# First expert pairs: order of the weight pieces on VectorE, and the tables of further visits on GpSimd

## The reference, cut to what matters

```python
def moe_swiglu(xn, router, wg, wu, wd):
    xt = xn.reshape(B * T, D)
    logits = (xt @ router).astype(F32)
    topv, topi = lax.top_k(logits, TOP_K)
    gates = jax.nn.softmax(topv, axis=-1)
    combine = jnp.sum(jax.nn.one_hot(topi, N_EXPERTS, dtype=F32) * gates[..., None], axis=1)
    y = jnp.zeros((B * T, D), F32)
    for e in range(N_EXPERTS):
        y = y + combine[:, e:e + 1] * swiglu(xt, wg[e], wu[e], wd[e]).astype(F32)
    return y.reshape(B, T, D).astype(xn.dtype)
```

## Time and profile before

| | |
|---|---|
| median of 3 runs | 2581.31 us |
| the profiled execution | 2579.01 us, its span 2577.2 us |
| TensorE matmul busy | 2502.2 us, 97% of the span |
| VectorE busy | 1932.0 us, 75% |
| ScalarE busy | 1492.6 us, 58% |
| GpSimd busy | 58.4 us, 2% |
| chain that ended last | PE 86%, DVE 8%, ACT 3%, DMA 2% |
| the 672 lo parts of L2306 | 798.3 us, 1226 ns each |
| the 672 hi parts of L2196 | 702.8 us, 1062 ns each |

### The profile page before, as it was taken

One profiled execution on the slowest core, in us unless ns is written; L12 is line 12 of the kernel. 1 busy time (PEld: TensorE's weight loads), 2 busy tenths in 40 slices (PEclk: granted clock), 3 DMA queues, 4 the chain that ended last, 5 costly groups with the idle time before them and its releaser, 6 DMA issues.

```text
span 2577.2 us, 41939 instructions
## 1 busy us (share of the span) xinstructions
PE 2502.2 (97%) x15981; PEld 2118.4 (82%) x15981; DVE 1932.0 (75%) x2704; ACT 1492.6 (58%) x2152; POOL 58.4 (2%) x32
## 2 busy tenths in 40 slices
PE   8899999989999999999999999999999999999998
PEld 7676998857888888888888888857999999866998
DVE  7855556758999999999999987877656655677555
ACT  5513434456888888888788885392443433356432
POOL 0100000000001010100001000000000000000000
PEclk9999999999999999999999999999999999999999
DMA  6655542587999999999999994203544552321551
GB/s 262 244 210 230 191 185 109 222 340 283 373 357 378 357 376 361 364 369 366 370 365 368 366 353 191 115 1 141 197 177 177 192 181 90 112 117 76 219 184 52
DMA packets 90971, 619.82 MB, mean 241 GB/s; under 512 B 10208, under 2 KB 10464, under 8 KB 40800
## 3 DMA queue, kind: packets, MB, share of 16 engines
q1 hardware_dynamic: 88992, 609.17, 61.5%
q0 software_dynamic: 1280, 4.72, 0.5%
q10 hardware_dynamic: 576, 4.19, 0.5%
HBM read 615.95 MB, written 2.10 MB: 240 GB/s over the span
## 4 chain that ended last, share of the span: by engine, by line
PE 86%; DVE 8%; ACT 3%; DMA 2%; issue 1%; DVEq 0%; SPq 0%; ACTq 0%
PE psum L1952 8%; PE psum L1954 8%; PE psum L1953 8%; PE psum L387 6%; PE psum L389 6%; PE psum L388 6%; PE psum L1989 4%; PE psum L1987 4%; PE psum L1988 4%; PE psum L402 3%; PE psum L403 3%; PE psum L404 3%; DMA ring<-stream_dram 2%; PE psum L1442 1%; PE psum L1961 1%; PE psum L2494 1%
## 5 line engine op out<-in xcount | busy, mean ns | idle before, releaser
L2306 DVE TENSOR_TENSOR r_high<-ring,r_high 128x1024 fp32r<-128x1024 f32 x672 | 798.3, 1226 | 56.6 <-ACT r_high L2196 43.6
L2196 ACT ACTIVATE r_high<-ring 128x1024 fp32r<-128x1024 f32 x672 | 702.8, 1062 | 75.9 <-PE psum L1954 49.7
L387 PE MATMUL psum<-r_low,r_high 128*128 128x256 f32 x1408 | 399.8, 284 | 1.5 <-DVE r_high L473 1.1
L389 PE MATMUL psum<-r_low,r_high 128*128 128x256 f32 x1408 | 398.4, 283 | 0.0
L1952 PE MATMUL psum<-r_high 128*128 128x512 f32 x896 | 359.1, 401 | 0.9 <-DVE r_high L2297 0.9
L1954 PE MATMUL psum<-r_high 128*128 128x512 f32 x896 | 349.8, 390 | 0.0
L1953 PE MATMUL psum<-r_high 128*128 128x512 f32 x896 | 349.4, 390 | 0.0
L473 DVE TENSOR_TENSOR r_high<-ring,r_high 128x1024 fp32r<-128x1024 f32 x264 | 307.1, 1218 | 9.5 <-ACT r_high L435 9.3
L388 PE MATMUL psum<-r_high 128*128 128x256 f32 x1056 | 298.8, 283 | 0.0
L447 ACT ACTIVATE arena<-psum 128x256 f32<-128x256 f32 x88 | 33.8, 384 | 441.0 <-PE psum L389 438.2
L387 PEld LDWEIGHTS psum<-r_low,r_high 128*128 128x128 f32 x1408 | 269.9, 192 | 6.6 <-DVE r_high L473 1.3
(11 more groups left out here) (603 smaller groups left out, 4468.5 us busy)
## 6 DMA issues: line engine op xcount, KB each, us to landing
ring<-stream_dram SPq DMA_DIRECT2D x160, 1536.0 KB, 6.5
ring<-stream_dram SPq DMA_DIRECT2D x224, 1024.0 KB, 6.8
ring<-stream_dram SPq DMA_DIRECT2D x224, 512.0 KB, 6.3
arena<-bias_dram ACTq DMA_DIRECT2D x2, 1024.0 KB, 7.7
pack<-pack_dram SPq DMA_DIRECT2D x1, 1664.0 KB, 16.9
const<-const_dram SPq DMA_DIRECT2D x1, 1060.0 KB, 13.4
x<-x_dram SPq DMA_DIRECT2D x1, 1024.0 KB, 4.9
xc<-ctx_dram ACTq DMA_DIRECT2D x1, 1024.0 KB, 6.2
```

Of the source, the lines that this page charges most:

```text
L387: pe.matmul(dst, hi, f["x_hi"][:, k, :], start=(k == 0), stop=False)
L389: ins = pe.matmul(dst, lo, f["x_hi"][:, k, :], start=False, stop=(k == KD - 1))
L2196: act.activation(dst, src, ACT.Copy).then_inc(sem("moe_w_hi"), 1)
L2306: ins = dve.tensor_tensor(lo, src, hi.bitcast(f32), SUB)
```

## The change

The function that makes lo parts is renamed to moe_split_lo, and takes any engine; it is still called for VectorE only. In moe_first_dve the order is new: own pieces 1 and 2, then both row operations, then xe_lo of half 0; and the product (moe_hidden_dve) stands behind pieces 0 and 1 of the next pair, with the next pair's pieces 2 and 3 and own pieces 4 and 5 behind it. The tables of further visits leave VectorE and are made by GpSimd ahead of its loop, with other operations: the sum over 8 experts as three additions in place of a reduction, one further visit at a time. VectorE waits for them once (pool_out) behind stage 13 of visit 0, and TensorE's wait for gathered rows counts one more (POOL_LRU).

```diff
@@ -1862,7 +1862,7 @@
         gates, chosen = tables[:, 272:280], tables[:, 280:296]
         ss_rest, root_bias = sm("ss_rest", 1), sm("root_bias", 1)
         xe_hi, xe_lo = [parts(27648 + D * i, D, "p (k s) -> p k s", k=KD) for i in range(2)]
-        AHEAD, POOL_LRU = 4, 2
+        AHEAD, POOL_LRU = 4, 3
         INDEX_AT, GATHER_AT = 6, 8
         x_rows = nc.dram_tensor("x_rows", (NT * P, D), f32).ap()
         slot_x = ar(0, D)
...
@@ -2095,7 +2095,7 @@
             add(1, 1)
             route_turned_dve(dve, 1)
             route_rows_dve(dve, 1, "norm_xn")
-            moe_split_dve(dve, moe_at(0, 0), 0, 0, 1)
+            moe_split_lo(dve, moe_at(0, 0), 0, 0, 1)
             route_choice_dve(dve, 1)
             best = top.rearrange("p (j e) -> p e j", j=NT)
             S(dve.tensor_tensor(gts[:, 2:4], best[:, 1, :], best[:, 0, :], SUB))
...
@@ -2258,6 +2258,8 @@
             pool.wait_ge(sem("norm_xn"), 4)
             pool.dma_start(x_rows.rearrange("(j p) d -> p j d", p=P), x_tm).then_inc(sem("moe_rows_in"), 16)
             moe_weights_pool(pool)
+            moe_more_visits_pool(pool)
+            moe_more_values_pool(pool)
             n_more = moe_more(pool)
             pool.wait_ge(sem("moe_rows_in"), 16)
             with pool.Fori(0, n_more) as v:
...
@@ -2296,14 +2298,14 @@
             dve.wait_ge(sem("moe_xe_hi"), half + 1)
             dve.tensor_tensor(xe_lo[:, ks, :], xe[:, ks, :], xe_hi[:, ks, :].bitcast(f32), SUB).then_inc(sem("moe_xe"), 1)
 
-        def moe_split_dve(dve, at, p, first=0, end=6):
+        def moe_split_lo(eng, at, p, first=0, end=6):
             r, turn, pair = at
             for q in range(first, end):
                 src = piece_of(r, q)
                 hi, lo = [steps_of(w[:, 0, :], 2 * q, 2) if q < 4 else d[:, 2 * (p % 2) + q - 4, :]
                           for w, d in ((wp_hi, d_hi), (wp_lo, d_lo))]
-                dve.wait_ge(sem("moe_w_hi"), 6 * pair + (q + 1))
-                ins = dve.tensor_tensor(lo, src, hi.bitcast(f32), SUB)
+                eng.wait_ge(sem("moe_w_hi"), 6 * pair + (q + 1))
+                ins = eng.tensor_tensor(lo, src, hi.bitcast(f32), SUB)
                 if q < 2:
                     ins.then_inc(sem("moe_w_lo"), 1)
                 elif q in (3, 5):
...
@@ -2353,54 +2355,56 @@
             S(pool.tensor_copy(token_of[:, :, 1], inv_rms[:, 0:2]))
             step(pool, pool.tensor_copy(gate_t[:, 0:2], vwgt[:, 0:2]), "moe_tables")
 
-        def moe_more_visits_dve(dve):
-
-            def S(ins, name="dve_step"):
-                step(dve, ins, name)
+        def moe_more_visits_pool(pool):
+
+            def S(ins, name="pool_step"):
+                step(pool, ins, name)
             iota8 = cst("iota")[:, 0:N_EXP]
             extra = MAX_VISITS - N_EXP
-            S(dve.tensor_tensor(rank, rank, over, SUB))
+            pool.wait_ge(sem("moe_plan"), 1)
+            S(pool.tensor_tensor(rank, rank, over, SUB))
             for n in range(extra):
-                S(dve.scalar_tensor_tensor(which[:, n, :], rank, float(n), over, ALU.is_equal, MUL))
-            S(dve.tensor_tensor(which_tmp[:, 0:extra, :], which, iota8.unsqueeze(1).to_broadcast([P, extra, N_EXP]), MUL))
-            S(dve.tensor_reduce(plan_f[:, 9:9 + extra], which_tmp[:, 0:extra, :], AX.X, ADD))
-            S(dve.tensor_copy(plan_f[:, 1:9], iota8))
-            S(dve.tensor_copy(plan_i[:, 1:12], plan_f[:, 1:12]), "moe_plan")
-
-        def moe_more_values_dve(dve, pairs):
-
-            def S(ins, name="dve_step"):
-                step(dve, ins, name)
+                S(pool.tensor_scalar(which[:, n, :], rank, float(n), None, ALU.is_equal))
+                S(pool.tensor_tensor(which[:, n, :], which[:, n, :], over, MUL))
+                S(pool.tensor_tensor(which_tmp[:, 0, :], which[:, n, :], iota8, MUL))
+                for e in (4, 2, 1):
+                    S(pool.tensor_tensor(which_tmp[:, 0, 0:e], which_tmp[:, 0, 0:e], which_tmp[:, 0, e:2 * e], ADD))
+                S(pool.tensor_copy(plan_f[:, 9 + n:10 + n], which_tmp[:, 0, 0:1]))
+            S(pool.tensor_copy(plan_f[:, 1:9], iota8))
+            S(pool.tensor_copy(plan_i[:, 1:12], plan_f[:, 1:12]), "moe_plan")
+
+        def moe_more_values_pool(pool):
+
+            def S(ins, name="pool_step"):
+                step(pool, ins, name)
             extra = MAX_VISITS - N_EXP
-            for dst, src in pairs:
-                for j in range(NT):
-                    S(dve.tensor_tensor(which_tmp[:, extra * j:extra * (j + 1), :], which,
-                                        src[:, :, j].unsqueeze(1).to_broadcast([P, extra, N_EXP]), MUL))
-                S(dve.tensor_reduce(dst[:, 2 * N_EXP:2 * MAX_VISITS].rearrange("p (n j) -> p j n", j=NT),
-                                    which_tmp.rearrange("p (j n) e -> p j n e", j=NT), AX.X, ADD))
-            if dst is vwgt:
-                S(dve.tensor_scalar(vpos[:, 2 * N_EXP:2 * MAX_VISITS], vpos[:, 2 * N_EXP:2 * MAX_VISITS], -float(CAP),
-                                    None, ADD))
+            for dst, src in ((vsel, sel), (vpos, pos), (vwgt, wgt)):
+                for n in range(extra):
+                    own = which_tmp[:, 0:NT, :]
+                    S(pool.tensor_tensor(own, which[:, n, :].unsqueeze(1).to_broadcast([P, NT, N_EXP]),
+                                         src.rearrange("p e j -> p j e"), MUL))
+                    for e in (4, 2):
+                        S(pool.tensor_tensor(own[:, :, 0:e], own[:, :, 0:e], own[:, :, e:2 * e], ADD))
+                    S(pool.tensor_tensor(dst[:, 2 * (N_EXP + n):2 * (N_EXP + n) + NT], own[:, :, 0], own[:, :, 1], ADD))
+            step(pool, pool.tensor_scalar(vpos[:, 2 * N_EXP:2 * MAX_VISITS], vpos[:, 2 * N_EXP:2 * MAX_VISITS], -float(CAP),
+                                          None, ADD), "pool_out")
 
         def moe_first_dve(dve):
 
             own, nxt = moe_at(0, 0), moe_at(0, 1)
-            moe_split_dve(dve, own, 0, 1, 2)
+            moe_split_lo(dve, own, 0, 1, 3)
             moe_xe_rows_dve(dve, 0)
-            moe_split_dve(dve, own, 0, 2, 3)
+            moe_xe_rows_dve(dve, 1)
             moe_xe_lo_dve(dve, 0)
-            moe_xe_rows_dve(dve, 1)
-            moe_split_dve(dve, own, 0, 3, 4)
+            moe_split_lo(dve, own, 0, 3, 4)
             moe_xe_lo_dve(dve, 1)
-            moe_split_dve(dve, nxt, 1, 0, 1)
-            moe_split_dve(dve, own, 0, 4, 5)
-            moe_split_dve(dve, nxt, 1, 1, 3)
+            moe_split_lo(dve, nxt, 1, 0, 2)
             moe_hidden_dve(dve, own)
-            moe_split_dve(dve, nxt, 1, 3, 4)
-            moe_split_dve(dve, own, 0, 5, 6)
+            moe_split_lo(dve, nxt, 1, 2, 4)
+            moe_split_lo(dve, own, 0, 4, 6)
             dve.wait_ge(sem("moe_h_hi"), 1)
             moe_hidden_lo_dve(dve)
-            moe_split_dve(dve, nxt, 1, 4, 6)
+            moe_split_lo(dve, nxt, 1, 4, 6)
 
         def moe_hidden_dve(dve, at):
             dve.wait_ge(sem("moe_silu"), at[2] + 1)
...
@@ -2427,10 +2431,8 @@
                         moe_pick_dve(dve, v + 1, p - 3)
                     if more and p in (5, 6):
                         moe_gate_dve(dve, v + 1, p - 5)
-                    if first and p == 7:
-                        moe_more_visits_dve(dve)
-                    if first and p in (8, 9, 10):
-                        moe_more_values_dve(dve, (((vsel, sel), (vpos, pos), (vwgt, wgt))[p - 8],))
+                    if first and p == PAIRS - 1:
+                        dve.wait_ge(sem("pool_out"), POOL_LRU)
                 if more:
                     moe_stage_dve(dve, moe_at(v, PAIRS), moe_at(v, PAIRS + 1), 0, out=v)
                 else:
```

More of the change, by code:

```diff
@@ L2313, in moe_stage_dve @@
             if nxt is not None:
-                moe_split_dve(dve, nxt, p + 1, 0, 3)
+                moe_split_lo(dve, nxt, p + 1, 0, 3)
             moe_hidden_dve(dve, at)
@@ L2319, in moe_stage_dve @@
             if nxt is not None:
-                moe_split_dve(dve, nxt, p + 1, 3, 5)
+                moe_split_lo(dve, nxt, p + 1, 3, 5)
             if out is not None:
@@ L2332, in moe_stage_dve @@
             if nxt is not None:
-                moe_split_dve(dve, nxt, p + 1, 5, 6)
+                moe_split_lo(dve, nxt, p + 1, 5, 6)
         def moe_out_dve(dve, v):
```

## The result

The changed kernel takes 2592.37 us, the median of 6 runs (2587.35 to 2595.13); the kernel before, measured beside it, 2581.30. The ratio is 1.0037, with a 95% interval from 1.0026 to 1.0047: by that ratio 9.6 us slower, by the medians 11.1. The forecast was 2581.4. The profiled execution took 2588.59 us with a span of 2586.8, against 2579.01 and 2577.2 before.

A forecast was written before the change was run, and what follows sets the result against it. VectorE was taken to pace the experts' first visit, with TensorE full almost everywhere after 612 us. Order +1.4, tables off VectorE -1.5 and GpSimd holding VectorE +0.2 summed to +0.1: 2581.4 us, range 2578.6 to 2592.0.

The forecast's parts named there:

- Part 3: Tables on GpSimd: 61 small operations done near 655, needed by 669.8, so cover 15 us and cost 0.
- the clock falls: Rival: the new 2.3 us TensorE hole could bring half clock for 3 us, costing 1.5: 2582.9; chance 0.05.
- Nine pieces between the products: VectorE, first to second pair's product: two pieces added make 9, 10.9 us instead of 8.6.
- Shift by the order 1.4: Part of the new moe_first_dve order: second pair's transposes 1.4 us later, and the shift stays 1.4.
- No further stall: Third pair: gate-up and TensorE both come 1.4 us later, so the shift does not grow.
- Tables off VectorE -1.5: Stage 7: without 3.08 us of tables the product precedes TensorE, closing the hole at 682.25; gain 1.5 us.
- GpSimd holding VectorE 0.2: Small GpSimd operations delay VectorE in the bound stretch 611 to 622: between 0 and 1.9 us, taken as 0.2.
- GpSimd done near 655: GpSimd's 61 table operations get in at ends of VectorE pieces, some 9 in 8.6 us, from 602.
- The sum of +0.1: Whole kernel: +1.4 for the order, -1.5 for the tables, +0.2 for GpSimd holding VectorE; 2581.4 us.
- The gather comes late: Rival: GpSimd tables finish near 680, delaying visit 1's gathered rows and TensorE's transposes by 10 us: 2591.5; chance 0.24.
- the forecast's own line of 5.2 us: A measurement tells 0.2% (5.2 us) from no change; chances faster 0.03, same 0.73, slower 0.24.
- three marks of being wrong: Second pair's transposes at 620 or before, a table operation beyond 670, or TensorE waiting for GpSimd at p = 8.

The follow-up runs named there:

- e1: The changed kernel with GpSimd's last visit-table operation raising moe_plan by itself, so each engine has its own count; ratio to the kernel before 1.0005.
- e5: The changed kernel with GpSimd's cast of the visit indices moved behind all but the last of the 37 value operations; ratio to the kernel before 1.0078.
- e9b: The changed kernel with 8 idle TensorE matmuls before the first gate-up and one before the first transposes; ratio to the kernel before 1.0032.
- e3: The kernel before with only the new order of moe_first_dve, tables still on VectorE; ratio to the kernel before 1.0011.
- e7: The kernel before with only the new order's second half, the first pair's product two pieces earlier; ratio to the kernel before 1.0011.
- e2: e1 with moe_first_dve in the old order, so only the tables move to GpSimd; ratio to the kernel before 0.9994.
- e4: e1 with another VectorE order: own pieces fill its waits, 7 pieces between the products; 2580.80 us, ratio to the kernel before 0.9996.
- e10: The kernel before with only idle TensorE matmuls around the gather and in the first pair's waits; ratio to the kernel before 0.9995.
- e4b: The same program as e4, measured again; ratio to the kernel before 0.9993.

## Why the prediction was wrong in its time and right in its parts

**The step that failed** is Part 3, "cover 15 us, cost 0", and with it the silence on new waits at the start. I priced GpSimd's 24 visit operations by who reads their results (far away, p = 8 and p = 13). The diff names the semaphore of the last of them, and that name was already used by VectorE in route_dve. The price is in the forecast's own numbers: the earlier trace rows give 0.20 and a step of 0.09 for a small operation, 7.0 us for 24, and VectorE waits until the 24 are done. The term was 0; it is +7.9 in the stage (7.87 of VectorE's idle; e1 takes it away, e5 enlarges it by 10.2).

**The second term of the miss** is the clock: the rival "the clock falls" had 0.05 and a price of 1.5. It came twice, 3.1 us in all. Against that, the gather's own slow clock (1.5, also in the earlier trace rows) costs nothing in the changed kernel, since VectorE is waiting anyway: the first gate-up stands 13.63 us behind the start of the gather with it and 13.64 without (e9b). Together +1.6, and 7.9 + 1.6 + 0.1 = 9.6.

**Right, point by point.**
- First gate-up 1.49 behind the gather's end: 1.58 in e3. (The terms of the forecast add up to 1.46, or 604.52.)
- First transposes 8.1 behind the gather's end (611.2): 8.26 in e3. The hole of 0.9: 0.93 in after, e1, e3.
- Nine pieces between the products, 10.9 us: 10.92, 10.94, 10.89, 10.88 in after, e1, e3, e7. Stall 2.3: 2.29, 2.30, 2.23, 2.25.
- Shift by the order 1.4: 1.52 at the second transposes, 1.85 over the stage. "No further stall" was a little off: in e3 the load behind own piece 5 is issued 12.92 us behind the gather's end (11.41 before, so 1.5 later, counted 1.4), ScalarE's wait for the third pair is 2.03 instead of 1.73, and the third transposes stand 9.27 instead of 9.04 behind the second.
- Tables off VectorE -1.5: -1.51 (e2), and -1.44 in after.
- GpSimd holding VectorE 0.2: 0.05 (e1 against e3), with pieces of 4.66 and 5.76 where the earlier trace rows have 4.63 and 5.76. It could have been 0.
- GpSimd done near 655, that is 57.3 behind the start of the gather: 55.8 in e2, 57.6 in e4, 48.6 in e1. In after it is 31.3: the visit tables ran undisturbed (0.24 to 0.32 apart) while VectorE stood still.
- The sum of +0.1: e1's ratio is 1.0005, +1.3 us (+2.6 by the medians), and its stage +0.3 once its falls of the clock are taken off, against e10, the kernel before without its fall.

One reading of the forecast is incomplete. It says that after the VectorE operation of 675.48 "the next ones went through" beside the large GpSimd operation of the earlier trace rows. One more of them was held to the end of it, in the same trace of before:

```profile
677.24 0.89 DVE L2367 COPY small<-const 128x8 f32<-128x8 f32 x1
```

The GpSimd operation ended at 678.09, this one at 678.13. The sum does not change by it. The chances of the forecast also count the late gather's 0.24 wholly as slower, although a part of it was to stay within 5.2 us.

**The rival that gives the right time for the wrong reason.** "The gather comes late" was priced at 2591.5, and after takes 2592.4. It did not happen. Its mark was TensorE waiting at p = 8, and there is no hole. The index is the last to come, not the tables (timeline of GpSimd after, with 48.10 us of idle before; the rows are scaled by 692.14 and the transposes of 693.76 need them):

```profile
629.54 1.10 POOL L2389 TENSOR_SCALAR pack<-pack 128x6 f32<-128x6 f32 x1
678.74 2.03 POOL L2268 DMA_INDIRECT arena<-x_rows,arena  x1 [48.10 <-DVE arena L2332]
687.55 4.59 POOL L2272 TENSOR_SCALAR arena<-arena 128x1024 f32<-128x1024 f32 x1 [6.78 <-DMA arena<-x_rows,arena]
```

Without the shared count too: in e1 the last table operation ended at 652.97 and the index came at 675.99. The agreement of 2591.5 and 2592.4 is a coincidence, and only the place in the trace tells.

**The range** went from 2578.6 to 2592.0. By the ratio the changed kernel stands at 2590.9, inside it; by its median, 0.4 beyond. That it is near at all is luck: the slow side was one case, cut in its middle, and that case did not happen. No case in it stood for a wait that the diff adds without showing it. By the forecast's own line of 5.2 us the change is slower, which had 0.24, all of it for the late gather.

Of the three marks of being wrong that the forecast names, none shows: the second transposes are not early, no table operation lies beyond 670, and TensorE does not wait for GpSimd at p = 8. What shows it is the first of the other marks, the first gate-up matmul: 13.63 us behind the start of the gather, where 604.5 meant 6.8.

## What to carry to other kernels

When work moves to another engine, look not only at who reads its results but at every semaphore that it signals, by name, and at how the target values are made: a counter kept while the program is built can make one engine wait for the other's event, and no line of the diff shows it. A filler between two deadlines of a saturated engine moves a stall rather than removing it: count the pieces between the two products, and compare with what TensorE needs. And judge a change of a few us by a distance inside the profile, with the granted clock beside it, since the clock's falls alone shift a run by 1.3 to 3.2.

## What the runs showed of the hardware

**Small GpSimd operations beside a saturated VectorE.** They get in once for each piece: in the changed kernel, beside the pieces of 620.99 and 625.91 above, they take 1.05 to 1.20 us instead of 0.20, while the pieces are not longer.

```profile
621.09 1.20 POOL L2384 TENSOR_TENSOR arena<-arena,pack 128x16 f32<-128x16 f32 x1
622.37 2.20 POOL L2387 TENSOR_TENSOR arena<-arena 128x8 f32<-128x8 f32 x2
624.65 1.05 POOL L2388 TENSOR_TENSOR pack<-arena 128x2 f32<-128x2 f32 x1
```

The large one of 4.59 us above is different from the other side: the four pieces that ran beside it took 5.47 instead of 4.63.

```profile
687.12 5.47 DVE L2308 TENSOR_TENSOR r_high<-ring,r_high 128x1024 fp32r<-128x1024 f32 x4 [0.24 <-ACT r_high L2196]
```

The Trainium skill (SBUF — State Buffer, section SBUF: two separate sides) says that a Vector operation with two SBUF inputs and a GpSimd operation that reads SBUF take an exclusive lock on a shared pair of ports, each for its whole instruction, and the other waits. For GpSimd waiting on VectorE the rows agree; for VectorE waiting on GpSimd they don't: by the rule none would have run beside it, and yet the four lost only 0.84 together beside an operation of 4.59.

**The clock's fall is not a function of the program.** e4 and e4b are one program: in one the gather took 5.43 us, in the other 3.81 and the first pair 1.6 more. A stall of 2.41 us in the earlier trace rows brought no fall; one of 2.40 at the same place in e2 made the second pair 1.5 longer (clock 0.72 in 612 to 618); one of 2.25 in e7 brought 6 us at 0.51. The Trainium skill (TensorE: Matmul & The Clock Gate, section What's actually happening) says that the number of slow matmuls varies from run to run of the same kernel. This pair agrees in that the slow matmuls are of the gather in one and of the first gate-up in the other; the cost of the fall is 1.6 us in both.
